# Closing matrix product of two gated layers: seven products over quarters for eight, on one Trainium2 core

## The chip, the cores and the metric

The kernel runs on one core of one Trainium2 chip. The metric is the device time of one execution in microseconds. TensorE (PE in the profile) does the matrix products, VectorE (DVE), ScalarE (ACT) and GpSimd (POOL) the elementwise work, and SyncE's queue (SP) issues every transfer. SBUF is the on-chip memory of the operands, PSUM the one into which TensorE writes: eight banks of 128 partitions x 512 floats, here three pairs S[0] to S[2] and one pair MM.

## The reference, cut to what matters

Two transformer blocks follow each other on 1024 tokens of 1024 channels, in float32. Each ends in a gated layer with a hidden width of 2816 = 22 x 128:

```python
def _swiglu(h, w_gate, w_up, w_down):            # first block
    return (jax.nn.silu(h @ w_gate) * (h @ w_up)) @ w_down
# x_new = x_new + g2 * _swiglu(h2, ...)          # g2: one factor for each channel

def conv_ffn(h, w_up, conv_w, conv_b, w_down):   # second block
    u = causal_dwconv(h @ w_up, conv_w, conv_b)
    g, val = jnp.split(u, 2, axis=-1)
    return (jax.nn.silu(g) * val) @ w_down
# x = x + conv_ffn(h, ...); the output is rmsnorm(x, final_norm_w)
```

After the first gated layer comes an RMS norm (factor from the mean of squares over the channels) and the second block's first projection; after the second one the last RMS norm and the output.

## The kernel before, in words

Everything is kept transposed: a tile is 128 channels x 1024 tokens. A float32 operand is split into a high part, rounded to the form in which TensorE multiplies at full pace (fp32r), and a low part, the difference. A product is then three matmuls of 128 x 128 weights by 128 x 512 values: high by high, low by high, high by low. ScalarE writes the high parts (`block_hi` for weights), GpSimd the low parts (`block_lo`).

The program is written out by hand for each engine, in `tensor_program`, `scalar_program`, `vector_program`, `gpsimd_program` and `sync_program`. Each engine runs its own list in order and waits on semaphores for named events, such as `made((f, n))`: block n of layer f is multiplied. So an instruction that waits holds up all that stands behind it on its engine.

A gated layer (`ffn`, with f = "f1" and "f2") has two stages. The first, the opening products, makes the hidden tiles; its weight blocks have the numbers 0 to NP-1, and from the third pair of rows on it already makes seven products over quarters for eight (`PROD`, `weight_sums`, `quarter_sum`). Hidden tiles go out to HBM (`store_hidden`). In f2 VectorE has the convolution's taps to add (`taps`), and after the last product those of the last pair still stand in its list. The second stage is the closing product: the 22 hidden tiles in six groups (`DNG`), for each group eight weight blocks, one for each output tile m. A block is 128 x 512 floats (128 x 256 in the group of two). Each hidden tile is loaded from HBM (`load_hidden`) and split (`hidden`, by VectorE, or for four tiles of f2 by ScalarE, and by GpSimd). TensorE (`down`) multiplies a block by both token halves, so that each output tile fills a pair of banks once in a group, and VectorE adds the pair to the tile `xt` of the running sum (`residual`). In all these are 22 x 8 x 2 x 3 = 1056 matmuls in each layer, all on line L871.

Weight blocks pass through a ring of six buffers: `block_hi` of block n waits for `made` of block n - 6. During the last group ScalarE squares each finished tile and GpSimd adds the squares up, except those of tile 7. Then `sum_squares` sums over the channels with a matrix of ones, in plain float32; ScalarE makes the factor (`rstd`: Ln, then Exp, half by half), and VectorE multiplies.

## Time and profile before

| | us |
|---|---|
| median of 3 runs | 2591.64 (2591.57 to 2594.48) |
| the profiled execution | 2597.92 |
| its span in the trace | 2595.0 |
| TensorE busy | 2525.9 (97%) |
| VectorE busy | 1455.8 (56%) |
| ScalarE busy | 984.4 (38%) |
| GpSimd busy | 1155.3 (45%) |

Busy times are shares of the span. TensorE's matmuls overlap, each row lasting longer than the distance to the next one, so its pace is read from start times or from counts in a stretch. An engine's idle time has the name of what released it. The profiled execution is 6.3 us above the median of the runs.

### The profile page before, as it was taken

The page shows a single profiled execution, that of the slowest core. Times are in us where ns is not written, and L with a number is a line of the kernel's source. Part 1 is how long each engine was busy: PE and PEld are TensorE (multiplying, and loading weights), DVE is VectorE, ACT ScalarE, POOL GpSimd, SP SyncE. Part 2 cuts the span into 40 slices and gives each one's busy share as a digit, 9 for nine tenths or more (in the row PEclk, how much of TensorE's full clock was granted, in tenths as well). Part 3 has the DMA queues.
Part 4 walks back from the last instruction along what each step waited for, and adds up shares of the span by engine and source line. Part 5 has one row for each costly group of instructions (what it writes and reads, how often), then busy time and mean ns, then how long its engine had stood idle before and what let it go on. Part 6 is the DMA issues. An engine that isn't in the chain of part 4 may idle for free.

```text
span 2595.0 us, 31637 instructions
## 1 busy us (share of the span) xinstructions
PE 2525.9 (97%) x12113; PEld 2033.0 (78%) x12113; DVE 1455.8 (56%) x1695; ACT 984.4 (38%) x1583; POOL 1155.3 (45%) x689
## 2 busy tenths in 40 slices
PE   7999999999999999999999999999999999999997
PEld 5778778887878888888887678777877788888886
DVE  4674278887176665654334211234189988875333
ACT  4652467877263233231113321234244444441113
POOL 0124122573476555555444211124476655556452
PEclk9999999999999999999999999999999999999999
DMA  7453010243312322233322011012412212235321
GB/s 294 130 194 82 23 50 18 70 109 129 98 57 86 109 82 90 81 126 134 102 78 106 33 35 46 25 33 73 138 41 77 99 69 94 85 118 171 104 78 65
DMA packets 71573, 235.81 MB, mean 91 GB/s; under 512 B 8945, under 2 KB 11121, under 8 KB 71298
## 3 DMA queue, kind: packets, MB, share of 16 engines
q1 hardware_dynamic: 71426, 233.80, 26.8%
q8 instruction: 98, 1.61, 0.3%
q14 instruction: 49, 0.40, 0.0%
HBM read 180.55 MB, written 39.85 MB: 85 GB/s over the span
## 4 chain that ended last, share of the span: by engine, by line
PE 85%; DVE 9%; ACT 2%; issue 2%; POOL 1%; DMA 0%; SPq 0%; DVEq 0%; ACTq 0%
PE S L871 18%; PE S L485 12%; PE S L486 11%; PE S L849 9%; PE S L853 9%; PE S L850 9%; PE MM L722 2%; PE S L722 1%; PE S L696 1%; DVE xt L1822 1%; PE S L697 1%; PE MM L710 1%; PE MM L488 1%; PE S L710 1%; PE S L504 1%
## 5 line engine op out<-in xcount | busy, mean ns | idle before, releaser
L2240 POOL TENSOR_TENSOR wbl<-rf,wbh 128x512 fp32r<-128x512 f32 (+1 forms) x352 | 517.1, 1474 | 446.7 <-ACT wbh L1264 446.5
L1264 ACT ACTIVATE wbh<-rf 128x512 fp32r<-128x512 f32 (+1 forms) x352 | 215.6, 619 | 677.9 <-PE S L871 353.8
L2117 POOL TENSOR_TENSOR wl<-raw,wh 128x1024 fp32r<-128x1024 f32 x59 | 148.3, 2516 | 558.8 <-ACT wh L1028 558.8
L849 PE MATMUL S<-th_t,wbh 128*128 128x512 f32 x640 | 251.7, 393 | 0.9 <-DVE ub L1869 0.6
L853 PE MATMUL S<-tl_t,wbh 128*128 128x512 f32 x640 | 251.1, 392 | 0.0
L850 PE MATMUL S<-th_t,wbl 128*128 128x512 f32 x640 | 250.5, 391 | 0.0
L871 PE MATMUL S<-fl,wbh 128*128 128x512 f32 x704 | 219.6, 391 | 1.6 <-POOL fl L2264 1.6
L871 PE MATMUL S<-fh,wbh 128*128 128x512 f32 x704 | 220.4, 392 | 0.0
L871 PE MATMUL S<-fh,wbl 128*128 128x512 f32 x704 | 219.9, 392 | 0.0
L485 PE MATMUL S<-hh,wh 128*128 128x512 f32 (+1 forms) x456 | 195.2, 428 | 13.1 <-DVE gt L2046 3.1
L849 PE MATMUL S<-th_b,wbh 128*128 128x512 f32 x480 | 189.6, 395 | 2.7 <-DVE cu L1866 1.9
L1772 DVE SCALAR_TENSOR_TENSOR xt<-S,mv,xt 128x1024 f32<-128x1024 f32 (+1 forms) x58 | 72.3, 1247 | 212.4 <-PE S L871 151.8
L1774 DVE TENSOR_TENSOR xt<-S,xt 128x1024 f32<-128x1024 f32 (+1 forms) x58 | 68.8, 1187 | 216.9 <-PE S L871 145.5
L853 PE MATMUL S<-tl_b,wbh 128*128 128x512 f32 x480 | 188.5, 393 | 0.0
L850 PE MATMUL S<-th_b,wbl 128*128 128x512 f32 x480 | 187.8, 391 | 0.0
L485 PE MATMUL S<-hl,wh 128*128 128x512 f32 (+1 forms) x456 | 178.2, 391 | 3.6 <-POOL hl L2231 1.5
L486 PE MATMUL S<-hh,wh 128*128 128x512 f32 (+1 forms) x456 | 179.7, 394 | 0.0
L486 PE MATMUL S<-hh,wl 128*128 128x512 f32 (+1 forms) x456 | 179.6, 394 | 0.0
L485 PE MATMUL S<-hh,wl 128*128 128x512 f32 (+1 forms) x456 | 179.3, 393 | 0.0
L486 PE MATMUL S<-hl,wh 128*128 128x512 f32 (+1 forms) x456 | 178.9, 392 | 0.0
L871 PEld LDWEIGHTS S<-fl,wbh 128*128 128x128 f32 x704 | 131.9, 188 | 31.9 <-POOL fl L2264 3.3
L871 PEld LDWEIGHTS S<-fh,wbl 128*128 128x128 f32 x704 | 132.2, 188 | 29.6
(352 smaller groups left out, 5471.4 us busy)
## 6 DMA issues: line engine op xcount, KB each, us to landing
ff<-hid SPq DMA_DIRECT2D x44, 512.0 KB, 5.6
rf<-in_w_d SPq DMA_DIRECT2D x80, 256.0 KB, 2.7
mr<-in_w_modT SPq DMA_DIRECT2D x32, 512.0 KB, 5.1
rf<-in_w_f1g SPq DMA_DIRECT2D x22, 512.0 KB, 3.7
rf<-in_w_f1u SPq DMA_DIRECT2D x22, 512.0 KB, 3.3
hid<-pr SPq DMA_DIRECT2D x22, 512.0 KB, 2.6
rf<-in_w_f2g SPq DMA_DIRECT2D x22, 512.0 KB, 3.3
rf<-in_w_f2u SPq DMA_DIRECT2D x22, 512.0 KB, 3.3
```

The costliest lines, as they stand in the source:

```text
L485: e.matmul(S[j][0:mm, 0:512], lhs, x[:, k, 0:512], start=first, stop=last)
L486: i = e.matmul(S[j][0:mm, 512:1024], lhs, x[:, k, 512:1024], start=first, stop=last)
L722: i_ = e.matmul(TW[i % 2][:, 768:1024], vh[:, n % 2, v, :], pt[:, i % 2, :, x, :], start=x == 0, stop=x == nt - 1)
L849: e.matmul(o, hi[:, k, :], th[part][:, k, :], start=k == 0, stop=False)
L850: e.matmul(o, lo[:, k, :], th[part][:, k, :], start=False, stop=False)
L853: i = e.matmul(o, hi[:, k, :], tl[part][:, k, :], start=False, stop=k == 3)
L871: i = e.matmul(S[j][:, HALF[r]], wt[:, k, :], x[:, HALF[r]], start=first, stop=last)
L1264: e.activation(flat(wbh[wslot(f, n)][:, :, :])[:, 0:x.shape[1]], x, ACT.Copy).then_inc(*w_hi.mark((f, n)))
L1772: i = e.scalar_tensor_tensor(x, S[j][:, r], gate, x, ALU.mult, ALU.add)
L1774: i = e.tensor_tensor(x, S[j][:, r], x, ALU.add)
L2117: e.tensor_tensor(l, raw[:, w % 3, 0:n], h.bitcast(F), ALU.subtract).then_inc(*w_lo.mark(w))
L2240: e.tensor_tensor(l, x, h.bitcast(F), ALU.subtract).then_inc(*w_lo.mark((f, n)))
```

## The change

The closing product of each layer is made by seven products over quarters instead of eight. The 22 hidden tiles are taken in three groups of 8, 8 and 6 (`KT` pairs of 4, 4 and 3). In a group the weights are cut into four quarters (two halves of the outputs, two of the hidden tiles), and so are the values (two halves of the hidden tiles, two of the tokens). The step u runs over 3 x 7 products in the order `DOWN_ORDER`, and i over the four output tiles of one; a unit (u, i) is one weight block by one token half, 12 matmuls in the first two groups and 9 in the third. Products 1 and 2 take quarters as they are, products 5, 6, 7, 3 and 4 sums or differences on one side or both. VectorE makes the sums of weights (`weight_sum`) and of values (`part_sum`). Values are split two products ahead (`part_x_hi` on ScalarE, `part_x_lo` on VectorE, for products 1 and 3 on GpSimd), in chunks of two hidden tiles.

The eight banks hold one unit each: 0 to 3 for products 1, 2 and 6, 4 to 7 for 5, 3, 7 and 4. Products 2, 3 and 4 add to what the bank holds, after VectorE has read it (`evict`): they wait for `d_dn` of the product before. Product 1 of the first group is copied to a tile `u2` by ScalarE; `u2` gathers products 1 and 6 over the groups and is added to `xt` in the last group (`rest_u2`).

The squares of tiles 4 to 7 are no longer added by GpSimd: ScalarE squares them by token half, and TensorE sums all four with the matrix of ones, the second half of the tokens between units 1 and 2 of the last product (`square_sums(tag, 1)`), the first half after the last unit. In f2 the second half of the output is scaled and stored first (`out_half(1)`), and `out_half(1)` stands ahead of the last `evict` in VectorE's list.

```diff
@@ -41,13 +41,16 @@
 PROD = [None] * NF + [(q, p) for q in range(2, NPAIR) for p in ORDER]
 AT = {_p: _t for _t, _p in enumerate(PROD)}
 NP = len(PROD)
-DNG = [4, 2, 4, 4, 4, 4]
-GROUP = [_g for _g, _n in enumerate(DNG) for _ in range(_n)]
-DOWN = [(_g, _m) for _g in range(len(DNG)) for _m in range(8)]
+DOWN_ORDER = (1, 2, 5, 3, 6, 7, 4)
+KT = (4, 4, 3)
+A0 = (0, 8, 16)
+NU_ = 7 * len(KT)
+DOWN = [(_u, _i) for _u in range(NU_) for _i in range(4)]
+WQ = {1: 0, 2: 1, 5: 4, 3: 1, 6: 0, 7: 2, 4: 3}
 NB = NP + len(DOWN)
...
+    ph = [at(f"ph{z}", a, [128, 4, 512], R) for z, a in enumerate([AH + 16 * KB, V + 76 * KB, V + 92 * KB])]
+    pl = [at(f"pl{z}", a + 8 * KB, [128, 4, 512], R) for z, a in enumerate([AH + 16 * KB, V + 76 * KB, V + 92 * KB])]
+    xq_ = {c: at("xq" + c, a, [128, 4, 512], F) for c, a in
...
+        def down_bank(u, i):
+
+            x = i + (4 if DOWN_ORDER[u % 7] in (5, 3, 7, 4) else 0)
+            return S[x // 2][:, HALF[x % 2]] if x < 6 else M[x - 6][:, :]
...
+                def bank_free(u, i):
+                    p, g = DOWN_ORDER[u % 7], u // 7
+                    if p in (6, 7):
+                        return [(d_dn, (f, u - (3 if p == 6 else 2), i))]
+                    if g > 0:
+                        return [(d_dn, (f, u - (3 if p == 1 else 3), i))]
+                    x = i + (4 if p == 5 else 0)
+                    if x > 5:
+                        return ML.back[x - 6]
+                    return [y for t in range(NP - 6, NP) if t % 6 == x for y in given_up(f, t)]
+
+                for u, i in DOWN:
+                    n, p, g = down_at(u, i), DOWN_ORDER[u % 7], u // 7
+                    hi, lo, o = wbh[wslot(f, n)], wbl[wslot(f, n)], down_bank(u, i)
+                    fresh = p in (1, 5, 6, 7)
+                    if fresh:
+                        for signal_, event in bank_free(u, i):
+                            e.wait_ge(*signal_(event))
+                    elif p == 2 and g == 0:
+                        e.wait_ge(*a_cp((f, "u2", i)))
+                    else:
+                        e.wait_ge(*d_dn((f, u - 1, i)))
+                    e.wait_ge(*w_hi((f, n)))
+                    e.wait_ge(*w_lo((f, n)))
+                    for k in range(KT[g]):
+                        if i == 0:
+                            e.wait_ge(*a_th((f, "x", u, k // 2)))
+                        e.matmul(o, hi[:, k, :], ph[u % 3][:, k, :], start=fresh and k == 0, stop=False, skip_group_check=not fresh)
+                        e.matmul(o, lo[:, k, :], ph[u % 3][:, k, :], start=False, stop=False, skip_group_check=not fresh)
+                        if i == 0:
+                            e.wait_ge(*part_lo_done(f, u, k // 2))
+                        i_ = e.matmul(o, hi[:, k, :], pl[u % 3][:, k, :], start=False, stop=k == KT[g] - 1, skip_group_check=not fresh)
+                    i_.then_inc(*made.mark((f, n)))
+                    if u == NU_ - 1 and i == 0:
+                        SL.back = [[(d_dn, (f, u - 2, 0)), (d_dn, (f, u - 2, 1))], [(d_dn, (f, u - 2, 2)), (d_dn, (f, u - 2, 3))],
+                                   [(d_dn, (f, u, 0)), (d_dn, (f, u, 1))]]
+                        ML.back = [[(d_dn, (f, u, 2))], [(d_dn, (f, u, 3))]]
+                        SL.i = 0
+                        SL.take(e, tag, (a_ln, (tag, 0)))
+                        e.wait_ge(*p_x2((tag, 3)))
+                        for r in HALF:
+                            e.matmul(S[0][:, r], ONE, x2[:, r], start=True, stop=False)
+                    if u == NU_ - 1 and i == 1:
+                        square_sums(tag, 1)
+
+            def square_sums(tag, c):
+                for m in range(4, 8):
+                    e.wait_ge(*a_sq((tag, m, c)))
+                    i = e.matmul(S[0][:, HALF[c]], ONE, sqd[:, m - 4, HALF[c]], start=False, stop=m == 7)
+                i.then_inc(*summed.mark((tag, c)))
 
...
+            def part_x_hi(f, u, c):
+
+                g, p = u // 7, DOWN_ORDER[u % 7]
+                k0, k1 = chunks(u)[c]
+                e.wait_ge(*made((f, AT[NPAIR - 1, (5, 2, 6)[u]] if u < 3 else down_at(u - 3, 3))))
+                if p in (1, 2, 3):
+                    e.wait_ge(*l_hl(part_index(f, g, {1: 0, 2: 1, 3: 3}[p])))
+                else:
+                    e.wait_ge(*d_t((f, "sum", g, p, c)))
+                e.activation(ph[u % 3][:, k0:k1, :], part_raw(u)[:, k0:k1, :], ACT.Copy).then_inc(*a_th.mark((f, "x", u, c)))
...
+                        part_x_hi(f, 0, 0)
+                        part_x_hi(f, 0, 1)
+                part_x_hi(f, 1, 0)
+                part_x_hi(f, 1, 1)
...
+                for u, i in DOWN:
+                    n = down_at(u, i)
+                    if u == 0:
+                        e.wait_ge(*made((f, n)))
+                        e.activation(u2[:, i, :], down_bank(u, i), ACT.Copy).then_inc(*a_cp.mark((f, "u2", i)))
+                    block_hi(f, w0, n + RING)
+                    if u + 2 < NU_ and i < 2:
+                        part_x_hi(f, u + 2, i)
+                    if u == NU_ - 3 and i > 0:
+                        square_whole(out_tag, i - 1)
+                    elif u == NU_ - 2:
+                        if i == 0:
+                            square_whole(out_tag, 3)
+                            e.preload_act_table_set(LOG_EXP)
+                            e.wait_ge(*made((f, down_at(NU_ - 3, 3))))
+                        square_half(out_tag, i + 4, 1)
+                    elif u == NU_ - 1:
+                        square_half(out_tag, i + 4, 0)
+                        if i == 1:
+                            rstd_half(out_tag, rs2, 1)
...
+            def down(f, gate, out_half):
+
...
+                def evict(u, i):
+                    p, g = DOWN_ORDER[u % 7], u // 7
+                    if (p, g) == (1, 0):
+                        return
+                    e.wait_ge(*made((f, down_at(u, i))))
+                    o, done = down_bank(u, i), d_dn.mark((f, u, i))
+                    if p in (1, 6):
+                        e.wait_ge(*(a_cp((f, "u2", i)) if (p, g) == (6, 0) else d_dn((f, u - (4 if p == 6 else 3), i))))
+                        e.tensor_tensor(u2[:, i, :], o, u2[:, i, :], ALU.add).then_inc(*done)
...
+                def rest_u2(u, i):
+                    if u == NU_ - 3:
+                        e.wait_ge(*d_dn((f, u, i)))
+                        e.wait_ge(*d_dn((f, u - 1, i)))
+                        add(i, 1, u2[:, i, :], d_res.mark((f, "x", i)))
+                    elif u == NU_ - 2:
+                        e.wait_ge(*d_dn((f, u - 1, i)))
+                        e.wait_ge(*d_dn((f, u - 3, i)))
+                        add(i + 4, 1, u2[:, i, :], d_res.mark(("u2", f, i, 1)))
+                        e.wait_ge(*d_dn((f, u - 6, i)))
+                        add(i + 4, 0, u2[:, i, :], d_res.mark(("u2", f, i, 2)))
+
+                def weight_sum(g, p, i):
+                    w = slice(0, 128 * KT[g])
+                    a11, a12, a21, a22, s1 = (wq[c][i][:, w] for c in range(5))
+                    if p == 5:
+                        for c in (2, 3):
+                            e.wait_ge(*l_wq(quarter_index(f, g, c)))
+                        e.wait_ge(*(w_lo((f, down_at(7 * g - 5, i))) if g else made((f, NP - 1))))
+                        i_ = e.tensor_tensor(s1, a21, a22, ALU.add)
+                    elif p == 7:
+                        e.wait_ge(*l_wq(quarter_index(f, g, 0)))
+                        e.wait_ge(*d_s((f, g, 5, i)))
+                        i_ = e.tensor_tensor(a21, a11, a21, ALU.subtract)
+                    elif p == 6:
+                        e.wait_ge(*d_s((f, g, 7, i)))
+                        e.wait_ge(*w_lo((f, down_at(7 * g, i))))
+                        i_ = e.tensor_tensor(a11, s1, a11, ALU.subtract)
+                    else:
+                        e.wait_ge(*d_s((f, g, 6, i)))
+                        e.wait_ge(*w_lo((f, down_at(7 * g + 1, i))))
+                        i_ = e.tensor_tensor(a12, a12, a11, ALU.subtract)
+                    i_.then_inc(*d_s.mark((f, g, p, i)))
...
+                def part_x_lo(u, c):
+                    k0, k1 = chunks(u)[c]
+                    e.wait_ge(*a_th((f, "x", u, c)))
+                    e.tensor_tensor(pl[u % 3][:, k0:k1, :], part_raw(u)[:, k0:k1, :], ph[u % 3][:, k0:k1, :].bitcast(F),
+                                    ALU.subtract).then_inc(*d_tl.mark((f, "x", u, c)))
+
+                for c in range(2):
+                    part_x_lo(1, c)
+                for p in (5, 7, 6):
+                    for c in range(2):
+                        part_sum(0, p, c)
+                for u, i in DOWN:
+                    s, g = u % 7, u // 7
+                    if u == NU_ - 2:
+                        rest_u2(u, i)
+                    evict(u, i)
+                    if u == NU_ - 3:
+                        rest_u2(u, i)
+                    if s == 0:
+                        if g == 0:
+                            weight_sum(g, 5, i)
+                        else:
+                            weight_sum(g, 7, i)
+                    elif s == 1:
+                        if g == 0:
+                            weight_sum(g, 7, i)
+                        weight_sum(g, 6, i)
+                        weight_sum(g, 3, i)
+                    elif s == 6 and g < last:
+                        weight_sum(g + 1, 5, i)
+                    if i in (1, 2) and u + 2 < NU_ and (u + 2) % 7 not in (0, 3):
+                        part_x_lo(u + 2, i - 1)
+                    if s == 2 and i > 1:
+                        part_sum(g, 4, i - 2)
+                    elif g < last:
+                        if (s, i) in ((4, 3), (5, 0)):
+                            part_sum(g + 1, 5, 0 if i else 1)
+                        elif s == 5 and i > 1:
+                            part_sum(g + 1, 7, i - 2)
+                        elif s == 6 and i in (0, 3):
+                            part_sum(g + 1, 6, i // 3)
+                    if out_half is not None and u == NU_ - 1 and i == 2:
+                        out_half(1)
...
+            def out_half(c):
+                r = HALF[c]
+                e.wait_ge(*a_rs(("out", c)))
+                for k in range(8):
+                    if k < 4:
...
+                down(f, gate, out_half if f == "f2" else None)
...
+            def load_quarter(f, g, c):
+
+                half = c // 2
+                a = A0[g] + (KT[g] if c % 2 else 0)
+                if g == 0:
...
+                load_weights(f, 0, 0)
+                load_quarter(f, 0, 0)
+                load_quarter(f, 0, 1)
+                load_weights(f, 0, 1)
+                if f == "f2":
+                    load_x(f, 0)
+                    load_x(f, 1)
+                load_quarter(f, 0, 2)
+                load_quarter(f, 0, 3)
+                load_weights(f, 0, 2)
+                load_weights(f, 0, 3)
```

## Rows read from the trace of the kernel before

**Rows 1.** The page: busy time of each engine, and shares of the chain that ended last.
```profile
PE 2525.9 (97%) x12113; PEld 2033.0 (78%) x12113; DVE 1455.8 (56%) x1695; ACT 984.4 (38%) x1583; POOL 1155.3 (45%) x689
...
PE 85%; DVE 9%; ACT 2%; issue 2%; POOL 1%; DMA 0%; SPq 0%; DVEq 0%; ACTq 0%
```

**Rows 2.** Windows: stretch, length, busy PE, PEld, DVE, ACT, POOL (instructions), clock, DMA.
```profile
2100.00:2300.00 200.00, 200.00 (x872) 163.53 (x872) 173.84 (x165) 87.33 (x116) 111.41 (x73) 1.00 0.23 79
800.00:1150.00 350.00, 350.00 (x1523) 286.07 (x1523) 209.08 (x234) 108.76 (x184) 182.28 (x129) 1.00 0.25 87
1190.00:1390.00 200.00, 200.00 (x874) 163.88 (x873) 70.16 (x54) 27.00 (x42) 89.63 (x57) 1.00 0.31 100
1408.00:1440.00 32.00, 27.50 (x106) 13.98 (x105) 25.21 (x16) 14.45 (x17) 17.60 (x7) 0.95 0.14 51
...
2360.00:2560.00 200.00, 200.00 (x874) 163.93 (x873) 68.64 (x54) 31.63 (x46) 92.54 (x59) 1.00 0.26 84
```

**Rows 3.** Timeline of PE: start us, duration us; where both closing products begin and end.
```profile
1164.24 0.63 PE L871 MATMUL S<-fh,wbh 128*128 128x512 f32 x2
...
1407.50 1.88 PE L766 MATMUL S<-x,cst 128*128 128x512 f32 x4
1409.22 1.88 PE L769 MATMUL S<-sqt,cst 128*128 128x512 f32 x4
1410.93 4.05 PE L494 MATMUL S<-mlb,idb 128*128 128x512 bf16 x18
1416.82 0.39 PE L485 MATMUL S<-hh,wh 128*16 128x512 f32 x1 [1.84 <-ACT hh L1238]
...
2333.39 0.63 PE L871 MATMUL S<-fh,wbh 128*128 128x512 f32 x2
...
2576.49 1.88 PE L766 MATMUL S<-x,cst 128*128 128x512 f32 x4
```

**Rows 4.** Elementwise instructions by line: duration in ns, min/median/max, over the run.
```profile
L1755 DVE TENSOR_TENSOR rf<-rf,rf x40: 691/693/1678, 774.1 to 2306.8; 128x512 f32<-128x512 f32 x40
...
L1796 DVE TENSOR_TENSOR hl<-tt__156,hh x4: 1209/1210/1212, 1417.1 to 1434.1; 128x1024 fp32r<-128x1024 f32 x4
...
L2240 POOL TENSOR_TENSOR wbl<-s1t,wbh x40: 1271/1303/2177, 774.8 to 2307.5; 128x512 fp32r<-128x512 f32 x40
...
L2264 POOL TENSOR_TENSOR fl<-ff,fh x44: 2389/2406/3387, 1162.3 to 2524.5; 128x1024 fp32r<-128x1024 f32 x44
```

**Rows 5.** Timelines of DVE and POOL, 745 to 757 us: both working on SBUF at once.
```profile
753.19 1.67 DVE L1840 TENSOR_TENSOR tf_t<-tf_t,xt 128x512 f32<-128x512 f32 x1
...
745.83 15.29 POOL L2260 TENSOR_TENSOR tl_b<-xt,th_b 128x512 fp32r<-128x512 f32 x8
```

**Rows 6.** DVE groups between 2100 and 2300 us: count | busy us, mean ns | idle.
```profile
L1907 DVE SCALAR_TENSOR_TENSOR tg<-ub,vec,tg 128x1024 f32<-128x1024 f32 x20 | 40.0, 2020 | 0.4
L1907 DVE SCALAR_TENSOR_TENSOR tv<-ub,vec,tv 128x1024 f32<-128x1024 f32 x22 | 38.8, 1766 | 0.4
L1912 DVE TENSOR_TENSOR tv<-tv,tg 128x1024 f32<-128x1024 f32 x11 | 19.3, 1759 | 0.4
L1759 DVE TENSOR_TENSOR rf<-s1t,rf 128x512 f32<-128x512 f32 x10 | 13.1, 1314 | 0.0
```

**Rows 7.** Timeline of DVE where the closing products begin, f1 and then f2.
```profile
1166.23 2.18 DVE L1898 TENSOR_TENSOR pr<-pr,sg 128x512 f32<-128x512 f32 x1
...
2333.59 0.69 DVE L1875 TENSOR_TENSOR ub<-cu,S 128x512 f32<-128x512 f32 x1 [2.03 <-PE S L853]
2334.19 3.78 DVE L1907 SCALAR_TENSOR_TENSOR tv<-ub,vec,tv 128x1024 f32<-128x1024 f32 x2
...
2349.07 1.21 DVE L1774 TENSOR_TENSOR xt<-S,xt 128x1024 f32<-128x1024 f32 x1
```

**Rows 8.** DMA issues of the hidden tiles: count, KB each, median us to landing.
```profile
ff<-hid SPq DMA_DIRECT2D x44, 512.0 KB, 5.6
```

**Rows 9.** Timeline of DVE at the very end.
```profile
2582.70 8.03 DVE L2105 TENSOR_TENSOR xt<-xt,rs 128x1024 f32<-128x1024 f32 x7
```

356 lines of the change are left out of this document (197 added, 159 removed).

## The prediction

> **What bounds the kernel now.** First the page: TensorE is busy for 97% of the span and holds 85% of the chain that ended last, VectorE 9% [rows 1]. The next question is whether the two closing products share this bound. The windows inside them say so: in 1190 to 1390 us and in 2360 to 2560 us TensorE is busy for all 200 us, with 874 matmuls in each, at clock 1.00, while VectorE is at 70 and 69 us, ScalarE at 27 and 32, GpSimd at 90 and 93 [rows 2]. So one matmul costs 200/874 = 0.2288 us there, and three quarters of VectorE's and ScalarE's time is free. The timeline gives the ends: f1's product from 1164.24 to 1407.50, 243.26 us, and f2's from 2333.39 to 2576.49, 243.10 us, each 1056 matmuls and about 1 us of waits [rows 3]. The opening products already work in the new manner, seven of quarters: 872 matmuls in 200 us with VectorE at 174, and 1523 in 350 us (0.2298 us) [rows 2]. That is the nearest picture of the kernel to come.
>
> **The matmuls.** A layer gets 7 x 4 units x 11 pairs of hidden tiles x 3 = 924 matmuls for 1056. At 200/872 = 0.2294 us, the pace of f2's opening products [rows 2], they take 212.0 us. Against 243.26 and 243.10 that is 31.3 and 31.1 us less: **-62.4 us**.
>
> **The squares.** Before, both sums over channels stand behind the product: two matmuls on the collected squares from 1407.50 and two on tile 7 from 1409.22, 1.72 us for two, so 0.86 us each [rows 3]; plain float32 costs nearly four times a split one. Now two on the collected squares and four of the second token half stand between units of the last product: 6 x 0.86 = 5.2 us on TensorE's path in each layer, **+10.3 us**. Four more of the first half follow the last unit, as four did before; the first three can run while the last tile is read and squared.
>
> **The elementwise work, which lies beside the matmuls.** A layer has 84 weight blocks for 48, so ScalarE and GpSimd work harder, but the new load is VectorE's. An instruction with both operands in SBUF takes 0.69 us for 512 columns and 1.21 for 1024 when nothing disturbs it, one that reads PSUM 0.69 [rows 4, 7]. In a layer there are 80 reads of banks (55 us), 48 sums of weights, 16 of them of 384 columns (31), 24 sums of values (27), 30 low parts (34) and 12 additions of `u2` (8): 155 us in 194 instructions. A row overlaps the next by 0.08 us (2333.59 + 0.69 against 2334.19 [rows 7]), so it is 140 us of time. GpSimd: 56 low parts of 512 columns at 1.30 us, 28 of 384 at about 1.0, 10 of values (8 at 2.4, 2 at 1.3) and four squares (8): 131 us [rows 4]. To this comes what the two cost each other. Where both worked on SBUF without pause, VectorE's 0.69 became 1.67 and eight of GpSimd's took 15.3 us, 1.9 each for 1.3: they take turns [rows 5]. How often they meet is read in f2's opening products: the 42 taps, 11 products and 10 sums took 78.8, 19.3 and 13.1 us where 50.8, 13.3 and 6.9 would be due, 40 us lost in 200 beside 111 us of GpSimd, 0.36 us for each of GpSimd's [rows 2, 6]. I take this value, as that stage is the nearest: 0.36 x 131 = 47, so VectorE is occupied 187 us of 217. Bounds: 140 if they never meet, 140 + 114 x 1.0 = 254 if each of the 114 instructions on SBUF waits as in rows 5. ScalarE's load is near 100 us. So the middle of the stage costs nothing more; the cover is 30 us and is thin in places. VectorE's reading of products 1, 5 and 7 must end within three units, 8.3 us (6.2 in the last group), or products 2, 3 and 4 wait.
>
> The Trainium skill's page "SBUF — State Buffer", section "SBUF: two separate sides", calls this port an exclusive lock: VectorE with two SBUF inputs and GpSimd block each other for a whole instruction. By it nothing of the 1.67 us is shared bandwidth, and the sum by full blocking would be 254 us a layer, by the stage that I take 187. The trace agrees with the rule on the single instruction [rows 5], and rows 6 say that the meetings are rarer than that.
>
> **The start.** Here cover is missing. Unit times count from the stage's first matmul. The value quarters for product 1 can be asked for six products (16.7 us) ahead and hidden tiles land in 5.6 us each half megabyte under load [rows 8], so product 1 is ready. In f2 VectorE still has the taps of the last pair: before it was free 15.7 us after the first matmul (2349.07), and with fewer of GpSimd's large instructions against it I say 11.5 [rows 7]. Then come two low parts for product 2, wanted at 11.5 and there at 13 to 15: 2.3 us lost. Behind them stand six sums of values (8 to 13 us), and ScalarE's `part_x_hi(2, 0)` waits for the first of them; behind it on ScalarE stand the copies of `u2`, on which product 2's units 1 and 3 wait: about 3 us. The sums of weights for product 5 come after all six. Then the 12 sums of weights and 4 reads of product 2's round (9.6 us of its own, 12 to 14 with waits) stand ahead of the first read of product 5's bank, on which product 3 waits: about 3.5 us. Together 9 us, between 4 and 18. In f1 VectorE is free at about 4 us ([rows 7]: the last product of halves begins at 1166.23 and takes 2.2), and by the same list only the last of these waits is left: 1.5, between 0 and 8. **+10.5 us.**
>
> **The last group.** Units last 2.06 us there. In product 6's round VectorE has 4 reads, 4 additions of `u2` and two low parts while GpSimd has four blocks and the squares; it falls behind by some 3.5 us, and product 7's round adds 8 additions. In f2 ScalarE and GpSimd take turns over one squares buffer, 3.7 us a tile for four tiles, and TensorE waits for the fourth (`p_x2`) before the sum in unit 0. I take 1.5 us in f1 and 3.5 in f2, from 0 to 5 each: **+5.0 us.**
>
> **The tails.** In f1 5.9 us lay between the sums (1410.93) and the next product (1416.82): two Ln, two Exp, two products, two copies [rows 3]. One half of each is now done earlier: -2.5. In f2 18.5 us lay between the last matmul and the end of the span (2576.49 to 2595.0). Now `out_half(1)`, eight instructions of 0.61 us net, delays the last read to 4.5 us after the last matmul; square, sum, Ln and Exp bring it to 7.6, eight more half multiplications to 12.5 (the full ones ended at 2590.73 [rows 9]), and the last store takes the same 4.3: 16.8, so -1.7, say -2. **-4.5 us.**
>
> **Sum.** -62.4 + 10.3 + 10.5 + 5.0 - 4.5 = -41.1 us: the profiled execution goes from 2597.9 to about 2556.8, and as it stands 6.3 above the median, the median goes to 2550.5.
>
> **Rivals.**
> 1. The cover holds everywhere, starts and ends too. For it: f2's opening products ran at full pace with VectorE at 87% [rows 2]. Against it: the lists above name the late instruction. Stalls of 0 to 4 us instead of 15.5: 2535 to 2541.
> 2. VectorE becomes the bound in parts: it waits 0.7 us for each SBUF instruction instead of 0.41 (47/114), so it needs 140 + 80 = 220 us with its late starts on top, 228 in f1 and 236 in f2 where TensorE alone needs 217. For it: sums of weights and low parts are bunched into the rounds of products 2 and 4. Against it: GpSimd idles between blocks. This gives -15 - 7 - 4.5, up to -10: 2562 to 2582.
> 3. Slower: GpSimd and VectorE alternate all the time, the page's lock at its full price, 1.0 us for each of 114 instructions. For it: rows 5. Against it: rows 6. VectorE then needs 254 us, plus 10 at f2's start: +11 + 21 - 4.5, 2619. It decides from the wait at which a layer lasts 245 us, (245 - 140)/114 = 0.92 us for each instruction, more than twice what I take.
> 4. TensorE's own price: with waits of 2 to 4 us the clock could fall. After the wait of 1.84 us that ended at 1416.82 and the light matmuls before it [rows 3], the granted clock of 1408 to 1440 us was 0.95 [rows 2], a loss of some 1.6 us. Five such places are 8 us, within the range. The transfers are no rival: a group's loads have a whole group's time.
>
> **How the numbers follow.** My forecast, 2542 to 2561: 0.60. Rival 1: 0.10. Rival 2: 0.20. Rival 3 or a stall as large that I don't see: 0.10, of which 0.02 fall near no change. The likeliest time is 2551 us; the range of 8 in 10 is 2537 to 2580, leaving out half of rival 1 and all of rival 3. 0.2% is 5 us, about what a measurement can tell here. Faster by more than that 0.89, within it 0.02, slower 0.09.
>
> **What the profile after would show.** 924 closing matmuls a layer, 0.229 to 0.230 us apart between waits (right), more (a price of the form that I don't know). The stage from first to last closing matmul about 220 us in f1 and 231 in f2. TensorE's idle time in the first 45 us of f2's stage, released by VectorE's low parts, ScalarE's copy of `u2` and VectorE's reads, near 9 us. VectorE busy about 190 us of a stage; if it is above 210 and TensorE's waits on its reads are spread over all groups, rival 2 or 3 holds. Six sums of squares inside the last product at 0.86 us. Wrong would be the forecast if product 3 waits in every group, or if the low parts of weights come late because GpSimd is blocked.

## The result: 17 us faster, where 41 were forecast

The changed kernel took 2575.34 us (median of four, 2571.21 to 2579.3) beside 2592.47 for the kernel before on the same chip: ratio 0.9933, 95% interval 0.9914 to 0.9951. The time lies in the range (2537 to 2580), the gain is less than half of the forecast one. The profiled execution took 2573.28 us with a span of 2571.5. Its first closing matmul of f1 began 5.4 us earlier than before (1158.83 for 1164.24). That lies outside the change: in the trace of experiment 1, whose program is the same up to there, it began at 1164.42. So the spans overstate the gain, and the stages below are measured from their own first matmul. The changed kernel's profiled execution stands 2 us below its median.

The page of the changed kernel, busy time and chain, for [rows 1]:

```profile
PE 2476.3 (96%) x11873; PEld 1986.4 (77%) x11873; DVE 1688.9 (66%) x1952; ACT 1097.8 (43%) x1746; POOL 1253.4 (49%) x735
...
PE 81%; DVE 12%; issue 3%; ACT 2%; DMA 0%; POOL 0%; SPq 0%; DVEq 0%; ACTq 0%
```

TensorE is busy 49.6 us less, 240 records of matmuls fewer (264 split ones gone, 12 more on squares with two records each), but its share of the chain fell from 85 to 81% and VectorE's rose from 9 to 12%. The windows of the changed kernel (columns as in [rows 2]) show both whole closing stages, then the middle of each:

```profile
1158.80:1392.20 233.40, 221.44 (x938) 178.53 (x937) 208.49 (x195) 92.18 (x135) 166.62 (x95) 0.97 0.32 110
2318.60:2555.60 237.00, 219.83 (x938) 176.50 (x938) 212.51 (x203) 100.86 (x144) 169.68 (x95) 0.98 0.27 92
...
1220.00:1340.00 120.00, 120.00 (x525) 98.41 (x525) 104.29 (x103) 47.52 (x69) 91.36 (x53) 1.00 0.26 82
2380.00:2500.00 120.00, 120.00 (x526) 98.41 (x524) 100.34 (x100) 46.80 (x67) 92.84 (x52) 1.00 0.30 101
```

Read the last two first. In the middle TensorE never stops: 120/525 = 0.2286 us a matmul, with VectorE at 87 and 84% and GpSimd at 76 and 77%. The cover that the forecast called thin holds there. The time went elsewhere, and the timeline of TensorE shows where (start, duration, wait before it and what ended it):

```profile
1158.83 0.39 PE L925 MATMUL S<-ph,wbh 128*128 128x512 f32 x1
...
1201.49 0.79 PE L925 MATMUL S<-ph,wbh 128*128 128x512 f32 x1 [9.52 <-DVE xt L2073]
...
1377.05 0.75 PE L925 MATMUL S<-ph,wbh 128*128 128x512 f32 x1 [2.44 <-DVE xt L2073]
...
1384.59 3.60 PE L946 MATMUL S<-sqd,cst 128*128 128x512 f32 x8
1387.62 0.79 PE L925 MATMUL MM<-ph,wbh 128*128 128x512 f32 x1
...
1392.15 3.60 PE L946 MATMUL S<-sqd,cst 128*128 128x512 f32 x8
...
2318.64 0.39 PE L925 MATMUL S<-ph,wbh 128*128 128x512 f32 x1
...
2331.26 0.50 PE L929 MATMUL S<-pl,wbh 128*128 128x512 f32 x1 [0.95 <-DVE pl L2171]
2335.17 0.50 PE L925 MATMUL S<-ph,wbh 128*128 128x512 f32 x1 [1.34 <-ACT u L1500]
2342.06 0.50 PE L925 MATMUL S<-ph,wbh 128*128 128x512 f32 x1 [1.12 <-ACT u L1500]
2367.44 0.80 PE L925 MATMUL S<-ph,wbh 128*128 128x512 f32 x1 [11.39 <-ACT wbh L1342]
...
2542.00 0.50 PE L925 MATMUL S<-ph,wbh 128*128 128x512 f32 x1 [2.38 <-DVE xt L2075]
...
2555.55 2.74 PE L946 MATMUL S<-sqd,cst 128*128 128x512 f32 x6
2560.75 1.33 PE L946 MATMUL S<-sqd,cst 128*128 128x512 f32 x2 [2.47 <-ACT sqd L1291]
```

The large waits, 9.52 and 11.39 us, both stand before product 3 of the first group. Product 3 opens on product 5's banks. The view names ScalarE's weight rounding for the second one, but that block had been ready long before (GpSimd had ended its low part at 2356.30); the read of product 5's bank began at 2366.70 and the matmul followed 0.74 us later. By stage, the forecast being what its own terms add up to (for f2's first stretch its last paragraph says 231):

| stretch | before | forecast | after |
|---|---|---|---|
| f1, first closing matmul to the squares behind the last | 243.3 | 220.2 | 233.3 |
| f1, from there to the next product | 9.3 | 6.8 | 8.7 |
| f2, first closing matmul to the squares behind the last | 243.1 | 229.7 | 236.9 |
| f2, from there to the end | 18.5 | 16.5 | 15.95 |
| sum against before | | -41 | -19.3 |

This is VectorE's list in the first 42 us of f1's stage, in the changed kernel, as far as the read on which product 3 waits:

```profile
1159.75 1.80 DVE L2004 TENSOR_TENSOR pr<-pr,sg 128x512 f32<-128x512 f32 x1
1161.48 4.55 DVE L2171 TENSOR_TENSOR pl<-xq,ph 128x1024 fp32r<-128x1024 f32 x2
1165.95 2.35 DVE L2153 TENSOR_TENSOR xqt<-xq,xq 128x1024 f32<-128x1024 f32 x2
1168.22 2.35 DVE L2157 TENSOR_TENSOR xq<-xq,xq 128x1024 f32<-128x1024 f32 x2
1170.50 3.45 DVE L2161 TENSOR_TENSOR xq<-xq,xq 128x1024 f32<-128x1024 f32 x2
...
1181.85 0.74 DVE L2073 SCALAR_TENSOR_TENSOR xt<-S,mv,xt 128x512 f32<-128x512 f32 x1
1182.51 0.67 DVE L2134 TENSOR_TENSOR wq<-wq,wq 128x512 f32<-128x512 f32 x1
1183.22 1.67 DVE L2138 TENSOR_TENSOR wq<-wq,wq 128x512 f32<-128x512 f32 x1
1184.93 2.78 DVE L2142 TENSOR_TENSOR wq<-wq,wq 128x512 f32<-128x512 f32 x1
1187.63 0.74 DVE L2073 SCALAR_TENSOR_TENSOR xt<-S,mv,xt 128x512 f32<-128x512 f32 x1
...
1200.69 1.41 DVE L2073 SCALAR_TENSOR_TENSOR xt<-S,mv,xt 128x512 f32<-128x512 f32 x2
```

It has no pause. Product 2's round of four reads and twelve sums of weights, from 1181.85 to 1200.69, takes 18.8 us, 5.8 for each of two units and 3.7 for each of two more. And this is GpSimd in one of the slow units:

```profile
1182.67 1.67 POOL L2479 TENSOR_TENSOR wbl<-wq,wbh 128x512 fp32r<-128x512 f32 x1 [1.29 <-ACT wbh L1342]
1184.31 2.85 POOL L2504 TENSOR_TENSOR pl<-xq,ph 128x1024 fp32r<-128x1024 f32 x1
```

VectorE's 1.67 and 2.78 (0.69 each when undisturbed) both end 0.55 us behind an instruction of GpSimd's, at 1184.89 and 1187.71: each waited until GpSimd was through, and then ran. From 1161.5 to 1200.7 VectorE's 26 instructions with both operands in SBUF need 10 x 1.21 + 16 x 0.68 - 26 x 0.08 = 20.9 us of their own, its four reads of banks 4 x 0.66 = 2.6, and GpSimd's instructions (two large and ten small, at the undisturbed prices of [rows 4]) 4.8 + 13.0 = 17.8 us: together 41.3 us for the 39.2 that passed. So VectorE lost 15.7 us beside 17.8 us of GpSimd's work, nine tenths of it. The theory for the experiments: **in the first rounds the two engines take turns, and VectorE's list is nearly as long as the work of both.**

### The profile page after: what moved, and what is told of

It reads as the page before. It is cut to its first block, busy times and chain, and to the rows that moved or that the text cites. A ratio compares the mean times of both kernels' runs of the same rounds, so it can differ in the third digit from the quotient of the medians.

```text
span 2571.5 us, 32154 instructions
## 1 busy us (share of the span) xinstructions
PE 2476.3 (96%) x11873; PEld 1986.4 (77%) x11873; DVE 1688.9 (66%) x1952; ACT 1097.8 (43%) x1746; POOL 1253.4 (49%) x735
## 4 chain that ended last, share of the span: by engine, by line
PE 81%; DVE 12%; issue 3%; ACT 2%; DMA 0%; POOL 0%; SPq 0%; DVEq 0%; ACTq 0%
PE S L524 12%; PE S L525 11%; PE S L889 9%; PE S L893 9%; PE S L890 9%; PE S L925 3%; PE S L926 3%; PE S L929 3%; PE MM L761 2%; PE S L761 2%; PE S L735 1%; PE MM L926 1%; PE MM L925 1%; PE MM L929 1%; DVE xt L1928 1%
## 5 line engine op out<-in xcount | busy, mean ns | idle before, releaser
L2479 POOL TENSOR_TENSOR wbl<-rf,wbh 128x512 fp32r<-128x512 f32 x256 | 397.2, 1558 | 249.3 <-ACT wbh L1342 249.0
L2479 POOL TENSOR_TENSOR wbl<-wq,wbh 128x512 fp32r<-128x512 f32 (+1 forms) x168 | 277.6, 1662 | 118.8 <-ACT wbh L1342 118.8
L1342 ACT ACTIVATE wbh<-rf 128x512 fp32r<-128x512 f32 x256 | 158.5, 628 | 298.7 <-PE S L893 218.3
L1342 ACT ACTIVATE wbh<-wq 128x512 fp32r<-128x512 f32 (+1 forms) x168 | 99.5, 595 | 251.2 <-PE S L929 101.5
L925 PE MATMUL S<-ph,wbh 128*128 128x512 f32 x440 | 176.0, 400 | 28.2 <-DVE xt L2073 12.0
L926 PE MATMUL S<-ph,wbl 128*128 128x512 f32 x440 | 174.5, 397 | 0.0
L929 PE MATMUL S<-pl,wbh 128*128 128x512 f32 x440 | 173.4, 394 | 0.9 <-DVE pl L2171 0.9
L1090 ACT ACTIVATE wh<-raw 128x1024 fp32r<-128x1024 f32 x59 | 62.2, 1057 | 236.1 <-PE S L525 197.9
L889 PEld LDWEIGHTS S<-th_t,wbh 128*128 128x128 f32 x640 | 120.1, 188 | 27.9 <-DVE ub L1975 1.0
```

Source lines behind the costliest of these rows:

```text
L889: e.matmul(o, hi[:, k, :], th[part][:, k, :], start=k == 0, stop=False)
L925: e.matmul(o, hi[:, k, :], ph[u % 3][:, k, :], start=fresh and k == 0, stop=False, skip_group_check=not fresh)
L926: e.matmul(o, lo[:, k, :], ph[u % 3][:, k, :], start=False, stop=False, skip_group_check=not fresh)
L929: i_ = e.matmul(o, hi[:, k, :], pl[u % 3][:, k, :], start=False, stop=k == KT[g] - 1, skip_group_check=not fresh)
L1342: e.activation(flat(wbh[wslot(f, n)][:, :, :])[:, 0:x.shape[1]], x, ACT.Copy).then_inc(*w_hi.mark((f, n)))
L2479: e.tensor_tensor(l, x, h.bitcast(F), ALU.subtract).then_inc(*w_lo.mark((f, n)))
```

## The experiments

"Stage" is the stretch from the first closing matmul to 0.23 us after the start of the last, 233.3 and 236.9 us for the changed kernel. Ratios are to the kernel before, which had 2593.6, 2593.5 and 2592.6 us beside the experiments. Experiments 3, 4, 10 and 12 have one run each. The changed kernel's own four runs lie 8 us apart, and the intervals of experiments 1, 2, 5, 6 and 9 overlap its 0.9914 to 0.9951; so the argument goes by waits and stages read in the traces, and a median alone shows no gain of 3 to 7 us. Those of experiments 7, 8 and 11 lie clear of the changed kernel's.

**1. Six sums of values are two.** Do the sums that product 3 doesn't need lengthen the wait?

```
-                for p in (5, 7, 6):
-                    for c in range(2):
-                        part_sum(0, p, c)
+                for c in range(2):
+                    part_sum(0, 5, c)
...
                     evict(u, i)
+                    if u == 2 and i < 2:
+                        part_sum(0, 7, i)
+                        part_sum(0, 6, i)
```

> The four later sums of values of the first group (products 7 and 6) stand behind the reads of product 5's bank in VectorE's list instead of ahead of the sums of weights. Theory A, VectorE's list between the stage's first matmul and the read of product 5's bank is the long pole (39.2 us in f1 for 33.1 available): those four take 5.8 us in the changed kernel (2.35 + 3.45), so TensorE's wait before product 3 falls from 9.5 to about 4 us in f1 and from 11.4 to about 6 in f2, and the kernel gains 9 to 13 us. Rival B, the weights or values of product 3 come late by the transfers, or ScalarE's high part of its block is what is waited for: the waits stay and the time with them.

Measured: 2570.26 us, ratio 0.991 (0.9894 to 0.9926). The waits before product 3 fell from 9.52 and 11.39 us to 5.97 and 6.40; 0.99 us in f1 and 2.1 in f2 came back at later units, behind the moved sums. Stages 230.4 and 234.7. The sums were part of the list, and no transfer or weight held product 3 up. Four instructions of 5.8 us moved, and the two waits fell by 3.6 and 5.0; the median fell by 5 us, where 9 to 13 were expected.

**2. Filling matmuls before product 3.** What does the clock cost behind the wait?

```
                     fresh = p in (1, 5, 6, 7)
+                    if (u, i) == (3, 0):
+                        e.wait_ge(*d_dn((f, 1, 0)))
+                        idle(S[0], 36 if f == "f1" else 44)
```

> Matmuls on unused results fill TensorE's wait before product 3 of the first group, 36 in f1 (7.8 us) and 44 in f2 (9.5 us), with nothing moved. Theory C, a part of the missing gain is TensorE's clock after the long wait (granted 0.50 of full in the 4 us after f1's wait of 9.5 us, 0.58 after f2's of 11.4): the clock stays at 1.00 and each layer gains 2 to 3 us, 4 to 6 in all. If the clock costs nothing the time is that of the changed kernel, or above it by what the filling overruns.

Measured: 2570.38 us, ratio 0.9913 (0.9897 to 0.993). Product 3 began no earlier (42.7 us after the first closing matmul in both), but what followed it was quicker. The four microseconds behind the wait in f1, first the changed kernel:

```profile
1202.00:1206.00 4.00, 4.00 (x11) 3.04 (x10) 4.00 (x4) 1.43 (x3) 3.82 (x3) 0.50 0.23 66
```

and the filled one:

```profile
1201.20:1205.20 4.00, 3.99 (x17) 3.30 (x18) 4.00 (x4) 2.82 (x5) 3.79 (x3) 1.00 0.26 73
```

Clock 0.50 is 1.2 GHz of 2.4: 11 matmuls instead of 17. f1's stage was 3.5 us shorter (229.9), f2's 237.2. The 3.5 are two places. Behind product 3 eleven matmuls stood 0.43 us apart in the changed kernel and 0.23 here, which makes 2.3 us. At 1377 the changed kernel's clock was halved and this one's was not: eight matmuls cost 1.6 us more there, of which 1.2 reach the end of the stage. In f2 the filling saved 1.3 us behind product 3, and 1.6 were lost at 2537, where this time the filled kernel had the low clock. The expected gain was 2 to 3 us in each layer.

**3. GpSimd's low parts of product 3 on 8 columns.** They stand in the two slow units. This kernel leaves out most of the low parts of product 3's values in the first group.

```
+                w = 8 if u == 3 else 512
-                e.tensor_tensor(pl[u % 3][:, k0:k1, :], part_raw(u)[:, k0:k1, :], ...
+                e.tensor_tensor(pl[u % 3][:, k0:k1, 0:w], part_raw(u)[:, k0:k1, 0:w], ...
```

> GpSimd's two low parts of product 3's values in the first group work on 8 columns of each tile instead of 512; the rest of that low part is left out of the computation. They take 2.8 us each among VectorE's sums of weights. Theory D, VectorE's lateness is mostly waiting while GpSimd holds SBUF: the 12 sums and 4 reads of product 2's round (19.2 us from the first read to the read of product 5's bank in f1 for 9.6 of their own) shorten by 4 to 5 us, and so does TensorE's wait before product 3. Theory A alone, with the work itself as the length: by less than 1 us.

Measured, one run: 2565.58 us; the waits were 5.41 and 7.22 us. VectorE's list is unchanged, yet it ended 4.1 and 4.2 us earlier, as theory D said (4 to 5); theory A alone said less than 1.

**4. Twelve sums of weights on 8 columns.** This kernel leaves out most of the sums of weights for products 7, 6 and 3 in the first group.

```
-                    w = slice(0, 128 * KT[g])
+                    w = slice(0, 8 if g == 0 and p != 5 else 128 * KT[g])
```

> The 12 sums of weights for products 7, 6 and 3 of the first group work on 8 columns instead of 512; the rest of these sums is left out of the computation. Theory A: with them gone from the list (12 of 1.7 us with waits) TensorE's wait before product 3 is gone in f1 and at most 2 us in f2, the clock stays at 1.00, and the kernel gains 22 to 28 us. If a wait of several us stays before product 3, something else was as late as VectorE.

Measured, one run: 2564.94 us; the waits were 4.00 and 4.93 us, where none and at most 2 us were expected, and the clock behind them was 0.50 for the expected 1.00. Both waits were still ended by VectorE's read of product 5's bank. The timeline of VectorE says why:

```profile
1183.38 1.29 DVE L2138 TENSOR_TENSOR wq<-wq,wq 128x8 f32<-128x8 f32 x1
1184.70 2.33 DVE L2142 TENSOR_TENSOR wq<-wq,wq 128x8 f32<-128x8 f32 x1
...
1193.53 0.17 DVE L2142 TENSOR_TENSOR wq<-wq,wq 128x8 f32<-128x8 f32 x1
```

and that of GpSimd:

```profile
1183.35 1.29 POOL L2479 TENSOR_TENSOR wbl<-wq,wbh 128x512 fp32r<-128x512 f32 x1 [1.29 <-ACT wbh L1342]
1184.61 2.40 POOL L2504 TENSOR_TENSOR pl<-xq,ph 128x1024 fp32r<-128x1024 f32 x1
```

A sum of 8 columns takes 0.17 us alone, but 1.29 or 2.33 us when GpSimd is at work, and ends with GpSimd's instruction, to 0.03 us. The price of a meeting is what is left of GpSimd's instruction, whatever VectorE wants to do. The Trainium skill's page "SBUF — State Buffer", section "SBUF: two separate sides", says this of its exclusive lock, that each engine waits for the other's whole instruction; these rows agree, and no shared speed is seen in them.

**5. Product 2's low parts in the opening products.**

```
                     if t == NP - 4:
                         part_x_hi(f, 0, 0)
                         part_x_hi(f, 0, 1)
+                    if t == NP - 3:
+                        part_x_hi(f, 1, 0)
+                        part_x_hi(f, 1, 1)
...
+                    if t in (NP - 3, NP - 2):
+                        part_x_lo(f, 1, t - NP + 3)
```

> Edit: the rounded parts and the low parts for product 2 of each layer's closing stage (VectorE, two instructions on 128x1024, 4.55 us together in the first layer after the change) are made during the last three opening products instead of behind all of them; nothing else moves. Theory A (the waits ahead of product 3 are the length of VectorE's list from its last opening product to its read of product 5's bank): the list becomes 4.5 us shorter, the wait of 9.52 us in the first layer falls to 4.5 to 6 us, the one of 11.39 us in the second to 6.5 to 8 us, the one of 0.95 us ahead of product 2 in the second layer goes away, and the median falls from 2575.3 us to 2564 to 2569 us. Rival B (VectorE is as late in the opening products, so that the moved work only makes the closing stage start later): the first closing matmul starts 3 to 5 us later against the first opening product of its layer, and the time stays within 2 us of 2575.3 us.

Measured: 2572.1 us, ratio 0.9915 (0.9901 to 0.993). A miss: the waits stayed at 9.38 and 11.37 us; stages 233.8 and 238.2, both longer than the changed kernel's. The 0.95 us went away, but the next wait in f2 grew from 1.34 to 2.04. VectorE of this kernel at the end of f1's opening:

```profile
1154.41 3.46 DVE L2070 TENSOR_TENSOR pl<-xq,ph 128x1024 fp32r<-128x1024 f32 x1
...
1159.49 2.31 DVE L2070 TENSOR_TENSOR pl<-xq,ph 128x1024 fp32r<-128x1024 f32 x1
```

The two went in where the changed kernel's VectorE had only 0.55 and 0.42 us of pause, met GpSimd there (3.46 and 2.31 for 1.21), and pushed the opening's last products back. Here, moving work forward within a full list won nothing. The closing stage did not start later (1157.55), so rival B failed in its own form too.

**6. Both ends.** The half of the output behind the last read, and four additions of `u2` in product 4's round.

```
-                    if out_half is not None and u == NU_ - 1 and i == 2:
+                    if out_half is not None and u == NU_ - 1 and i == 3:
...
                         add(i + 4, 1, u2[:, i, :], d_res.mark(("u2", f, i, 1)))
-                        e.wait_ge(*d_dn((f, u - 6, i)))
+                    else:
+                        e.wait_ge(*d_dn((f, u - 7, i)))
                         add(i + 4, 0, u2[:, i, :], d_res.mark(("u2", f, i, 2)))
```

> Edit: in the last round of the second layer the scaling and storing of the output's half 1 stands behind VectorE's last read of a bank instead of ahead of it, and in the last rounds of both layers the four additions of the spare accumulator into half 0 stand in product 4's round instead of product 7's. Theory A (the three waits of 2.44, 2.38 and 2.47 us at the ends are VectorE's list order): the waits ahead of product 4's second unit (2.44 and 2.38 us) fall below 0.5 us each, the last read of a bank in the second layer comes 1 to 1.5 us after the last matmul instead of 3.8 us, the stretch from the last matmul to the end of the second layer falls from 15.95 us to 13 to 15 us, and the median falls by 4 to 7 us, to 2568 to 2571 us. Rival B (the additions moved into product 4's round make the last reads late instead, or the half moved behind the last read runs into the other half): two of the three waits come back at another place and the median falls by less than 2 us.

Measured: 2568.77 us, ratio 0.9903 (0.9889 to 0.9918). The waits of 2.44 and 2.38 us became 1.23 and 1.16, with 0.66 and 0.62 on GpSimd's collected squares behind them, not the 0.5 at most that were expected. So of the 1.2 us won at each wait more than half came back. f2's last stretch is 1.2 us shorter (14.8). Stages 231.6 and 236.5; some 1.2 us of f1's 1.7 are the clock, which was 1.00 behind this wait and 0.57 in the changed kernel. These make 3.3 us of the 6.6 between the medians; the rest lies within the intervals.

**7. and 8. All four edits, without and with filling.** Experiments 1, 5 and 6 together; then 12 and 14 filling matmuls before product 3.

> Edit: the sums of parts for products 7 and 6 of the first group behind the reads of product 5's bank, product 2's low parts in the opening products, and both edits at the ends, together. Theory A (all are the order of VectorE's list, and add up): the waits ahead of product 3 fall to 0.5 to 3 us in the first layer and to 1 to 4 us in the second, the granted clock does not fall to half behind them, the waits at the ends go, and the median is 2556 to 2562 us. Rival B (the weights' way through VectorE, ScalarE and GpSimd is what ends product 3's wait once the banks are read earlier): the waits stay above 4 us, ended by the weights of product 3, and the median is 2563 us or more.

> Edit: as the kernel with all four edits, and 12 and 14 filling matmuls, whose results nothing uses, ahead of product 3 in the first and second layer. If the waits left there are 3 us or more and the clock falls behind them, the filling keeps it at 1.00 and the time is 1 to 3 us below that of the kernel with all four edits; if the waits left are under 2 us, the clock does not fall anyway, the filling stands in the way of the matmuls behind it, and the time is 1 to 3 us above.

Measured: 2564.48 us, ratio 0.9884 (0.9867 to 0.99), and 2566.0 us, ratio 0.9893 (0.9879 to 0.9908). Without filling, waits of 4.24 and 6.12 us, both ended by the read of product 5's bank, and a clock of 0.50 behind both: the sum was expected too low (2556 to 2562), because experiment 5 gives nothing. With filling the waits were still 3.48 and 3.13 us, the clock behind them was 0.63 and 0.57 all the same, and nothing was gained, where 1 to 3 us were expected.

**9. and 10. Who makes the low parts.** The test of the theory. In 9 VectorE makes product 3's low parts of the first group instead of GpSimd. In 10 GpSimd makes product 5's instead of VectorE.

```
-            return (p_tl if DOWN_ORDER[u % 7] in (1, 3) else d_tl)((f, "x", u, c))
+            return (p_tl if DOWN_ORDER[u % 7] in (1, 3) and u != 3 else d_tl)((f, "x", u, c))
...
-                    if i in (1, 2) and u + 2 < NU_ and (u + 2) % 7 not in (0, 3):
+                    if i in (1, 2) and u + 2 < NU_ and ((u + 2) % 7 not in (0, 3) or u == 1):
                         part_x_lo(u + 2, i - 1)
```

> Edit: the low parts of product 3's values in the first group of each layer (two instructions on 128x1024) are made by VectorE instead of GpSimd, at the same place of the round; nothing else moves. VectorE has more to do, GpSimd less. Theory C (in the first rounds the two engines take turns on SBUF, so that the sum of both engines' work sets the time; 1.21 us on VectorE takes the place of 2.41 on GpSimd, twice): the wait ahead of product 3 falls by 2 to 3 us in each layer, from 9.52 and 11.39 to 6.5 to 7.5 and 8.5 to 9.5, and the median by 3 to 6 us from 2575.3. Theory L (VectorE's own list is what is late, and its lost time is the same for each instruction): two more instructions make the waits 2 to 3.5 us longer each, 12 and 14 us, and the median 2579 to 2583.

> Edit, the mirror of the one above: the low parts of product 5's values in the first group (two instructions on 128x1024) are made by GpSimd instead of VectorE. Theory C: 2.41 us on GpSimd in the place of 1.21 on VectorE, twice, makes the waits ahead of product 3 up to 2.4 us longer, 10.5 to 12 in the first layer. Theory L: VectorE's list is shorter by 2.4 to 3.5 us, and the waits fall to 6 to 7 us in the first layer and to 8 to 9 in the second.

Measured for 9: 2570.76 us, ratio 0.9913 (0.9898 to 0.9927); waits 6.62 and 8.64 us, 2.9 and 2.75 shorter, with more work on the late engine. One unit of product 2's round in it:

```profile
1184.48 0.74 DVE L2073 SCALAR_TENSOR_TENSOR xt<-S,mv,xt 128x512 f32<-128x512 f32 x1
1185.14 0.68 DVE L2134 TENSOR_TENSOR wq<-wq,wq 128x512 f32<-128x512 f32 x1
1185.86 1.67 DVE L2138 TENSOR_TENSOR wq<-wq,wq 128x512 f32<-128x512 f32 x1
1187.56 0.69 DVE L2142 TENSOR_TENSOR wq<-wq,wq 128x512 f32<-128x512 f32 x1
1188.17 1.22 DVE L2171 TENSOR_TENSOR pl<-xq,ph 128x1024 fp32r<-128x1024 f32 x1
1189.31 0.74 DVE L2073 SCALAR_TENSOR_TENSOR xt<-S,mv,xt 128x512 f32<-128x512 f32 x1
```

4.8 us with the low part in it, for 5.8 without; the round took 15.9 us for 18.8. For 10, one run: 2575.51 us; in f1 a wait of 9.37 us, in f2 3.32 (on a copy of `u2`) and 7.03, and product 3 began 42.8 and 49.2 us after the first closing matmul, where it was 42.7 and 48.8. Taking 2.4 us of work off the late engine gained nothing. The single list (theory L) falls by both. Theory C has 9 on the number. In 10 it expected up to 2.4 us of loss and there was next to none. The trace shows f1 in two parts: product 2's round began 2.3 us earlier against the first closing matmul, and then took 21.3 us for 18.8. Some of the moved work went into pauses of GpSimd's (4.5 and 3.6 us in the changed kernel). Reckoned as above from VectorE's first low part to the read of product 5's bank, it lost 15.7 us beside 17.8 of GpSimd's in the changed kernel, 10.5 beside 13.0 in 9 and 18.1 beside 22.6 in 10: always most of it, eight to nine tenths, and never all. What lets the rest go by was not shown.

**11. The best one.** Experiments 1, 6 and 9 together.

> Edit: the sums of parts for products 7 and 6 of the first group behind the reads of product 5's bank, both edits at the ends, and product 3's low parts of the first group on VectorE. Theory C: the waits ahead of product 3 are 3 to 4 us in the first layer and 3.5 to 4.5 in the second, and the median is 2557 to 2562 us. Theory L: they are 8 us or more each, and the median is 2568 us or more.

Measured: 2558.4 us (2556.83 to 2560.52), ratio 0.9868 (0.9851 to 0.9885): 34.2 us faster than before, twice the gain of the change. Waits and median are where theory C said. Its waits and its two stages:

```profile
1194.30 0.79 PE L925 MATMUL S<-ph,wbh 128*128 128x512 f32 x1 [3.09 <-DVE xt L2073]
...
2349.95 0.50 PE L925 MATMUL S<-ph,wbh 128*128 128x512 f32 x1 [4.08 <-DVE xt L2075]
```

```profile
1158.10:1384.90 226.80, 220.89 (x938) 177.50 (x937) 205.61 (x197) 91.90 (x135) 161.60 (x93) 0.98 0.32 113
2309.90:2540.30 230.40, 220.36 (x937) 176.37 (x936) 206.71 (x202) 100.29 (x144) 165.38 (x93) 0.99 0.27 95
```

f2's stage is at the 230 that was forecast for the change, f1's still 6.6 above its 220.

**12. Fewer squares.** TensorE's sums leave out the squares of tiles 4, 5 and 6.

```
-                for m in range(4, 8):
+                for m in (7,):
```

> Edit: TensorE's sums of squares take tile 7 and the collected tiles 0 to 3 alone; tiles 4, 5 and 6 are left out of both halves' sums in both layers, which takes away six float32 matmuls a layer, three of them inside the last product. If one costs 0.86 us on TensorE's path, as forecast, each layer's stretch from the first to the last closing matmul is 2.6 us shorter (230.7 us in the first layer for 233.3, 234.3 in the second for 236.9), and the tails are 0 to 2.6 us shorter as well. If instead they fill time in which the last product waits anyway, the stretches stay within 0.7 us of 233.3 and 236.9.

Measured, one run: 2572.77 us; stages 232.8 and 236.4, only 0.5 and 0.6 shorter. The sum of tile 7 then waits for ScalarE's square:

```profile
1386.40 1.78 PE L946 MATMUL S<-sqd,cst 128*128 128x512 f32 x2 [2.29 <-ACT sqd L1291]
```

So the three others cost TensorE nothing that it could have used: at that place it would have waited for tile 7's square.

## Why the gain was less than half of the forecast one

**The matmuls: right.** 0.2286 us each in the middle of both stages, 0.2294 forecast.

**The squares: right in size.** 1384.59 to 1387.62 is 3.03 us for four, and the first matmul behind them is 0.40 us longer to its successor than usual: 3.4/4 = 0.86 us. The six take 5.2 us a layer. Experiment 12 adds that the way of tile 7 through VectorE and ScalarE stands behind the three others at nearly the same length: without their 2.6 us TensorE waited 2.29.

**The start waits: the step that failed.** They were put at 1.5 us in f1 and 9 in f2, and measured 9.5 and 14.8: 13.8 of the miss. Not the beginning was wrong: VectorE was free 2.7 us after the first matmul in f1 and 10.3 in f2, where 4 and 11.5 were said. The waits of 0.95, 1.34 and 1.12 us before product 2's units fall short of the forecast 5.3. What failed is the sentence on product 2's round, "9.6 us of its own, 12 to 14 with waits": it took 18.8 and 18.5 us, so 5 to 7 of the 8.0 us that f1 missed by. The rest came ahead of it, where fourteen instructions lost 6.7 us in f1. The forecast took the mean rate at which the engines meet, 0.41 us for each instruction on SBUF, over the whole stage. In that round the own time is 12 x 0.69 + 4 x 0.74 - 16 x 0.08 = 10.0 us, so twelve such instructions lost 8.8 us, 0.73 each; that is rival 2's rate, at the place that rival 2 named, the bunched sums of weights. Experiments 3, 4 and 9 show the cause: in that round GpSimd has its own two large low parts and four blocks, 10.0 us, and the round lasts nearly as long as both engines' work. Over the stage VectorE was occupied 208 us in f1 for the 187 forecast, (208 - 140)/114 = 0.60 us lost for each instruction on SBUF, and 213 in f2. The mean rate was too low too, but only in the first group and, for 2.4 us, in the last one did TensorE wait for it. So rival 2 (2562 to 2582, 0.20) has the time and the rate, but not its form: VectorE was not what a whole stage lasts by.

**The clock: left out of the sum, and it came.** 2.3 us behind f1's wait and 1.3 behind f2's, shown by experiment 2, and 1.2 at 1377. It stood outside the sum, as rival 4, at 1.6 us a place.

**The last group: right in sum, in part by luck.** 5.0 us forecast, 2.44 and 2.38 measured. Both stand before product 4's second unit and are VectorE's lateness, as said for f1. The wait on the fourth square (`p_x2`), for which f2 was given 2 us more, was not seen in either layer; experiment 6 laid it open behind the shortened wait, at 0.66 and 0.62 us. The same experiment shows that half of each wait was the order of the additions.

**The tails: f2 right in sum (-2.6 for -2), f1 not (-0.65 for -2.5).** In f1 VectorE's second product of the half meets GpSimd's low parts of the next weights; the timeline of VectorE, then that of GpSimd:

```profile
1397.17 2.84 DVE L1888 SCALAR_TENSOR_TENSOR tt__156<-xt,vec,rs 128x512 f32<-128x512 f32 x1 [3.40 <-ACT rs L1298]
```

```profile
1394.79 4.67 POOL L2356 TENSOR_TENSOR wl<-raw,wh 128x1024 fp32r<-128x1024 f32 x2 [14.83 <-ACT wh L1090]
```

0.74 us of work takes 2.84. But the same meeting stood there before the change, where two products took 3.31 us for 1.4; VectorE and GpSimd of the kernel before:

```profile
1412.71 3.31 DVE L1782 SCALAR_TENSOR_TENSOR tt__156<-xt,vec,rs 128x512 f32<-128x512 f32 x2 [4.26 <-ACT rs L1232]
```

```profile
1410.14 4.67 POOL L2117 TENSOR_TENSOR wl<-raw,wh 128x1024 fp32r<-128x1024 f32 x2 [3.00 <-ACT wh L1028]
```

So 1.9 us were lost before and 2.1 after, and the meeting is no new cost. What the forecast had too large is the saving: one half of each step done earlier took only 0.4 us from Ln and Exp and 0.5 from the products, and ScalarE began 0.2 us later. No run moved these instructions, so this is a reading of the two traces alone. In f2 two misses cancel: the last half multiplications ended 13.1 us after the last matmul for the forecast 12.5, and what followed them took 2.9 us for 4.3.

Together: 8.0 + 5.8 (start waits), 3.5 + 1.3 (clock), 0.9 - 1.1 (last group), 1.9 - 0.6 (tails) are 19.7 of the 21.7 us between forecast and stages; the other 2.0 us were not traced. The likeliest time missed by 24; what lies between that and the stages is other parts of the program and the spread of the runs.

## What to carry to other kernels

A mean rate of collisions does where there is cover (it was too low here over the whole stage, and cost nothing in the middle), and fails in the round where both engines' work is bunched: write out the first round of a pipeline, both engines' lists side by side, and add them up. Where VectorE has no pause, add to its list what GpSimd does meanwhile; here eight to nine tenths of it came on top. Giving the late engine a share of the early one's work gained here, because it does the same work in half the time (1.21 us for 2.41). Before an instruction is moved forward, look for a pause in the list where it lands. And look whether a meeting stood there before the change too, before the miss is put down to it.

## What the runs showed of the chip that was not expected

The granted clock after a wait of TensorE is not the same from one execution to the next. The wait of 2.37 to 2.44 us before product 4's second unit stands in both layers of nine kernels (the changed one and experiments 1 to 5, 9, 10 and 12): in 11 of 18 places the clock of the next 4 us was 0.57 to 0.62, and the next matmuls cost some 1.6 us more; in 7 it was 1.00. Two such windows of the changed kernel, the same place in f1 and f2:

```profile
1377.05:1381.05 4.00, 4.00 (x10) 3.14 (x11) 4.00 (x3) 1.04 (x2) 2.91 (x2) 0.57 0.00 0
2542.00:2546.00 4.00, 4.00 (x14) 2.66 (x15) 4.00 (x4) 2.64 (x4) 3.07 (x2) 1.00 0.01 2
```

Behind the waits of 1.16 to 1.23 us of experiments 6, 7, 8 and 11 it was 1.00 in all eight places, behind those of 3.09 us and more inside the closing stages 0.50 to 0.65 every time. A wait of 2.04 us in f2 of experiments 5 and 7, before product 2's second unit, was followed by 1.00 in one and 0.63 in the other. From product 4's wait to the end of the stage the low clock made f1 1.2 us longer and f2 about 1.5, so executions of one kernel can differ by this alone by nearly 3 us.
